# Gated delta rule in a decoder trunk: key and query norms as per-token factors, symmetric decayed products, and the next tile's front spread over the levels of this tile

## What is computed

```python
q = l2_norm(q) * (128 ** -0.5);  k = l2_norm(k)
g = cumsum(g) within the chunk                      # one decay per token and head
decay = exp(where(incl, g_i - g_j, -inf))
kb = k * beta
lower = where(strict, kb @ k.T * decay, 0)
rhs = concat([v * beta, kb * exp(g)])
u, w = triangular_solve(eye + lower, rhs)
attn = q @ k.T * decay
# over the chunks, S is the state (128 x 128 per head)
v_new = u - w @ S
o = (q * exp(g)) @ S + attn @ v_new
S = S * exp(g_last) + (k * exp(g_last - g)).T @ v_new
# then
o = rms_norm(o, onorm_w) * silu(z)
```

## Time and profile before

| | us |
|---|---|
| median of 3 runs (lowest, highest) | 2449.37 (2445.22, 2451.26) |
| the profiled execution's own time | 2451.56 |
| its span, first to last instruction | 2449.7 |
| PE busy | 2210.4 (90%) |
| DVE busy | 1598.6 (65%) |
| ACT busy | 1259.7 (51%) |
| POOL busy | 457.5 (19%) |
| mean granted TensorE clock, share of full speed | 0.949 |

### The profile page before, as it was taken

The page is one execution under the profiler, slowest core; times in us unless marked ns, Lnnn a source line. Parts: engine busy times, 40 slices in busy tenths (PEclk is TensorE's granted clock), DMA queues, the critical chain, the costliest instruction groups (busy, mean ns, idle before and its releaser), DMA issues. The chain is left out here.

```text
span 2449.7 us, 36342 instructions
## 1 busy us (share of the span) xinstructions
PE 2210.4 (90%) x10361; PEld 1679.8 (69%) x10361; DVE 1598.6 (65%) x2553; ACT 1259.7 (51%) x2072; POOL 457.5 (19%) x343
## 2 busy tenths in 40 slices
PE   7989688877999999999999399999999998999992
PEld 6867667776667776777777265567676776777771
DVE  3768754455578877788777321434777777888883
ACT  3332122122347777787776112322477776777871
POOL 0000322230013322232222000000132222322220
PEclk9999899998999999999999599699999999999996
DMA  5221000000469999999998502013699999999993
GB/s 190 87 86 39 18 1 1 1 1 19 173 225 376 373 360 348 359 376 367 361 357 289 172 26 69 1 39 132 230 366 340 365 351 342 372 364 372 372 348 94
DMA packets 177844, 536.68 MB, mean 219 GB/s; under 512 B 25856, under 2 KB 55520, under 8 KB 177632
## 3 DMA queue, kind: packets, MB, share of 16 engines
q1 hardware_dynamic: 147568, 457.50, 49.5%
q0 software_dynamic: 25248, 69.25, 11.3%
q10 hardware_dynamic: 4944, 8.84, 1.0%
HBM read 501.56 MB, written 54.07 MB: 227 GB/s over the span
## 5 line engine op out<-in xcount | busy, mean ns | idle before, releaser
L1322 DVE TENSOR_TENSOR gu_l<-ring,gu_h 128x1024 fp32r<-128x1024 f32 x512 | 611.3, 1221 | 99.5 <-ACT gu_h L1208 90.6
L1208 ACT CAST gu_h<-ring 128x1024 fp32r<-128x1024 f32 x512 | 523.3, 1058 | 91.7 <-DMA ring<-in_moe_w_up 74.3
L1140 PE MATMUL bank<-gu_h,xgT_l 128*128 128x512 f32 x1024 | 413.5, 404 | 0.0
L1142 PE MATMUL bank<-gu_h,xgT_h 128*128 128x512 f32 x1024 | 401.7, 392 | 0.0
L1141 PE MATMUL bank<-gu_l,xgT_h 128*128 128x512 f32 x1024 | 400.7, 391 | 0.0
L1450 POOL DMA_INDIRECT xg<-h_rows,list_idx x128 | 143.4, 1120 | 836.7 <-issue 318.2
L1179 PE MATMUL bank<-ring,hmT_f 128*128 128x512 f32 x544 | 279.3, 595 | 0.0
L1468 POOL DMA_INDIRECT moe_sum<-y,out_idx x128 | 216.1, 1688 | 220.2 <-issue 212.7
L1215 ACT CAST down_h<-ring 128x1024 fp32r<-128x1024 f32 x130 | 136.2, 1047 | 213.4 <-PE bank L1179 116.2
L1328 DVE TENSOR_TENSOR down_l<-ring,down_h 128x1024 fp32r<-128x1024 f32 x130 | 159.4, 1226 | 99.9 <-ACT down_h L1215 97.9
L1142 PEld LDWEIGHTS bank<-gu_h,xgT_h 128*128 128x128 f32 x1024 | 193.2, 189 | 42.6
(11 more groups left out here) (301 smaller groups left out, 3531.3 us busy)
## 6 DMA issues: line engine op xcount, KB each, us to landing
ring<-in_moe_w_gate SPq DMA_DIRECT2D x256, 512.0 KB
ring<-in_moe_w_up SPq DMA_DIRECT2D x256, 512.0 KB
ring<-in_moe_w_down SPq DMA_DIRECT2D x256, 512.0 KB
ring<-in_a_w_in SPq DMA_DIRECT2D x32, 512.0 KB
ring<-in_a_w_out SPq DMA_DIRECT2D x8, 512.0 KB
h_rows<-ring ACTq DMA_DIRECT2D x8, 512.0 KB, 2.7
moe_sum<-y ACTq DMA_DIRECT2D x8, 512.0 KB, 7.4
ring<-moe_sum SPq DMA_DIRECT2D x8, 512.0 KB, 5.5
```

Source lines behind the costliest of these rows:

```text
L1140: nc.tensor.matmul(out, lhsT=xl, rhs=wh, start=k == 0, stop=False)
L1142: last = nc.tensor.matmul(out, lhsT=xh, rhs=wh, start=False, stop=k == KD - 1)
L1208: nc.scalar.copy(gu_h[:, c, :, :], gate_up_cols(gate_slot, c * CH // 2, CH // 2)).then_inc(gu_hi.sem, 1)
L1322: nc.vector.tensor_tensor(gu_l[:, c, :, :], gate_up_cols(gate_slot, c * CH // 2, CH // 2), gu_h[:, c, :, :].bitcast(F32), ALU.subtract).th ...
```

## The change

The norms of q and k are no longer applied to q and k.

- The 16 `sum_squares` all add into one bank: a shifted row of one 1 as weights puts the sum of head c in row c. They are issued two after each of the first 8 z steps. One DVE copy, four PE transposes and a few operations on 128x32 or 128x64 elements give per token and head `k_gain` (beta over the sum), `k_norm` (root of the sum), `q_gain2` and `q_gain`. The 128x512 roots, reciprocals and scalings are gone.
- Decay is exp(-|g_i - g_j|), which is symmetric, so S = k k^T times decay serves as lower part and as its transpose, and the q by k product is made transposed at once (keys are the weights, key and query the 256 moving columns). The four transposes per group of L694 and L695 and the copies L759, L760 are gone. `k_gain` enters as a factor of rows (a matmul, `gain_rows`) and of columns, in `weighted`, and in the diagonal, in place of the identity (`diagonal`, on POOL). v is scaled by `k_norm`, the output by `q_gain` in `dve_gated`.
- X and Y of the next tile, and all that leads to them, are made during this tile: keys' transposes behind level 0, `gate_rows` behind level 1, `keys_queries` in two halves behind levels 2 and 3, `gain_rows` behind level 4, `first_X` and `first_Y` between the steps of the scan. Only tile 0 has a front of its own.
- Column sums of the decays are made once for all tiles (`cols`).
- In the scan, q by state stands ahead of the wait for v_new, four matmuls in a row, and attn by v_new follows as four in a row.
- POOL's order in a tile, two groups each, is now: `decay_queries`, mask 2, `scale_values`, mask 3, `upper_part` of the next tile, mask 4, `diagonal` of the next tile, then for each chunk c the decay of the state and mask c of the next tile. These are 22 operations a tile where there were 18.
- Semaphores that are no longer there for later blocks are shared with those of this one.

The diff, cut to its core (the removed PE, ACT, DVE and POOL programs of the block stand in the kernel above):

```diff
@@ gdn_projections, ScalarE
-                for c in range(2 * H + 1):
-                    if c < 2 * H:
-                        if c >= 2:
-                            act.wait_ge(side_ready.sem, side_ready.base + H + c - 1)
-                        nc.scalar.activation(squares[:, c % 2, :], qkT[:, c, :], ACT.Square).then_inc(squared.sem, 1)
-                    if c >= 1:
...
-                        nc.scalar.activation(norm[:, (c - 1) % 2, :], bank[6 + (c - 1) % 2][:, :], ACT.Sqrt, bias=eps_col[:, 0:1]).then_inc(norm_done.sem, 1)
+                for c in range(2 * H):
+                    if c >= 2:
+                        act.wait_ge(sums_ready.sem, sums_ready.base + c - 1)
+                    nc.scalar.activation(squares[:, c % 2, :], qkT[:, c, :], ACT.Square).then_inc(squared.sem, 1)
+                act.wait_ge(sums_copied.sem, sums_copied.base + 2)
+                nc.scalar.activation(k_norm[:, :, :], sum_cols[:, :, H:], ACT.Sqrt)
+                act.wait_ge(sums_copied.sem, sums_copied.base + 3)
+                nc.scalar.activation(q_gain[:, :, :], q_gain2[:, :, :], ACT.Sqrt, scale=float(P))
@@ gdn_projections, TensorE, behind each z step
-                    sum_squares(n)
+                    if n < H:
+                        if n == 0:
+                            pe.wait_ge(eps_set.sem, eps_set.base + 4)
+                        sum_squares(2 * n)
+                        sum_squares(2 * n + 1)
+                    elif n == H + 1:
+                        transpose_sums()
@@ gdn_projections, VectorE
-                for n in range(4 * TT + 1):
-                    if n < 4 * TT:
-                        copy_z(n)
-                    if n >= 1:
-                        normalise(n - 1)
+                for n in range(4 * TT):
+                    copy_z(n)
+                    if n == H:
+                        copy_sums()
+                    elif n == H + 2:
+                        norms()
@@ gdn_delta_rule, TensorE
+                def from_state(s, c):
...
+                    if c == 1:
+                        pe.wait_ge(vnew_done.sem, vnew_done.base + ev(s, 0) + 1)
+                    elif tt + 1 < TT:
+                        pe.wait_ge(w_scaled.sem, w_scaled.base + s + 3)
+                    for h in range(HG):
+                        last = nc.tensor.matmul(b[0][R, h * P:(h + 1) * P], lhsT=keg_wT[g][:, h, R], rhs=state[g][:, h, :], start=True, stop=True)
+                    last.then_inc(ws_ready.sem, 1)
...
+                    for h in range(HG):
+                        nc.tensor.matmul(b[3][R, h * P:(h + 1) * P], lhsT=qkT[:, HG * g + h, C], rhs=state[g][:, h, :], start=h == 0, stop=False)
+
+                def from_values(s, c):
...
+                    pe.wait_ge(vnew_done.sem, vnew_done.base + ev(s, c) + 1)
+                    for h in range(HG):
+                        nc.tensor.matmul(b[3][R, h * P:(h + 1) * P], lhsT=attnT[tt % 2][g][R, h, R], rhs=prod_vnew[g][R, h, :], start=False, stop=h == HG - 1)
+                    for h in range(HG):
+                        last = nc.tensor.matmul(b[1][:, h * P:(h + 1) * P], lhsT=k_dec[g][R, h, :], rhs=prod_vnew[g][R, h, :], start=True, stop=True)
+                    last.then_inc(scan_ready.sem, 1)
...
                 for tt in range(TT):
                     for level in range(LV):
+                        for s in both(tt):
+                            product(s, level)
+                        for s in both(tt):
+                            inverse(s, level)
+                        if level == 0:
+                            for s in both(tt):
+                                keys_T(s)
+                        elif tt + 1 < TT:
+                            for s in both(tt + 1):
+                                if level == 1:
+                                    gate_rows(s)
+                                elif level < 4:
+                                    keys_queries(s, level - 2)
+                                else:
+                                    gain_rows(s)
+                    for s in both(tt):
+                        values_keys(s)
+                    for c in range(2):
+                        for s in both(tt):
+                            from_state(s, c)
+                        for s in both(tt):
+                            from_values(s, c)
@@ gdn_delta_rule, ScalarE (decay(s) of the next tile follows the copies of level 2)
+                    nc.scalar.activation(eg_last[:, tt % 2, g, :, :], heads(b[0][:, :])[:, :, CHUNK - 1::CHUNK], ACT.Exp)
+                    nc.scalar.activation(eg_row[g][:, :, :], heads(b[0][:, :]), ACT.Exp)
+                    link(act, "act", nc.scalar.activation(sym[g], sym[g], ACT.Abs))
+                    nc.scalar.activation(sym[g], sym[g], ACT.Exp, scale=-1.0).then_inc(sym_done.sem, 1)
@@ gdn_delta_rule, VectorE
+                def decayed(s, half):
...
+                    v.wait_ge(kq_ready.sem, kq_ready.base + ev(s, half) + 1)
+                    v.wait_ge(sym_done.sem, sym_done.base + s + 1)
+                    both_of = kq_bank(s, half)[:, :].rearrange("p (h a q) -> p a h q", a=2, q=P)
+                    nc.vector.tensor_tensor(S[tt % 2][g][:, h, :], both_of[:, 1, :, :], sym[g][:, h, :], ALU.mult)
+                    v.wait_ge(upper_done.sem, upper_done.base + s + 1)
+                    nc.vector.tensor_tensor(attnT[tt % 2][g][:, h, :], both_of[:, 0, :, :], upper[g][:, h, :], ALU.mult).then_inc(kq_done.sem, 1)
+
+                def weighted(s):
...
+                    link(v, "dve", nc.vector.tensor_tensor(sym[g], heads(b_bank(s)[:, :]), S[tt % 2][g][:, :, :], ALU.mult))
+                    nc.vector.tensor_tensor(sym[g], sym[g], per_head(k_gain[:, tt, HG * g:HG * g + HG]), ALU.mult).then_inc(w_scaled.sem, 1)
+
+                def first_X(s):
...
+                    link(v, "dve", nc.vector.tensor_tensor(X[g][:, :, :], sym[g], planes(C_M0), ALU.mult))
+                    nc.vector.tensor_tensor(X[g][:, :, :], diag[g], X[g][:, :, :], ALU.subtract)
...
                     for c in range(2):
                         R = slice(c * CHUNK, (c + 1) * CHUNK)
+                        for s in both(tt):
+                            _, g, _, b = tile(s)
                             v.wait_ge(ws_ready.sem, ws_ready.base + ev(s, c) + 1)
+                            nc.vector.tensor_tensor(prod_vnew[g][R, :, :], v_tok[R, tt, HG * g:HG * g + HG, :], heads(b[0][R, :]), ALU.subtract).then_inc(vnew_done.sem, 1)
+                        if tt + 1 < TT:
+                            first_X(2 * tt + 2 + c)
+                        for s in both(tt):
+                            _, g, _, b = tile(s)
                             v.wait_ge(scan_ready.sem, scan_ready.base + ev(s, c) + 1)
                             v.wait_ge(state_decayed.sem, state_decayed.base + 2 + ev(s, c) + 1)
+                            nc.vector.tensor_tensor(state[g][:, :, :], sdec[g], heads(b[1][:, :]), ALU.add).then_inc(state_done.sem, 1)
+                        if tt + 1 < TT:
+                            first_Y(2 * tt + 2 + c)
@@ gdn_out, VectorE
-            nc.vector.tensor_scalar(o_rms[:, tt, :], o_rms[:, tt, :], 1.0 / P, EPS, ALU.mult, ALU.add).then_inc(rms_in.sem, 1)
+            nc.vector.tensor_tensor(o_rms[:, tt, :], o_rms[:, tt, :], q_gain2[:, tt, :], ALU.mult).then_inc(rms_in.sem, 1)
             v.wait_ge(rms_out.sem, rms_out.base + tt + 1)
             link(v, "dve", nc.vector.reciprocal(o_rms[:, tt, :], o_rms[:, tt, :]))
+            link(v, "dve", nc.vector.tensor_tensor(o_rms[:, tt, :], o_rms[:, tt, :], q_gain[:, tt, :], ALU.mult))
```

More of the change, by code:

```diff
@@ L661, in lev, with tile, both, kq_bank @@
             return 2 * per * tt + 2 * level + g
-        def banks(g):
-            return [bank[4 * g + i] for i in range(4)]
+        def tile(s):
+            tt, g = divmod(s, 2)
+            return tt, g, slice(tt * P, (tt + 1) * P), [bank[4 * g + i] for i in range(4)]
+        def both(tt):
+            return [2 * tt, 2 * tt + 1]
+        def kq_bank(s, half):
+            return tile(s)[3][1 + half if s < 2 else 0]
+        def b_bank(s):
+            return tile(s)[3][3 if s < 2 else 0]
+        def per_head(ap):
+            return ap.unsqueeze(2).to_broadcast([P, HG, P])
         with nc.Block(name="gdn_delta_rule") as block:
@@ new lines, in keys_queries @@
+                def keys_queries(s, half):
+                    tt, g, tok, b = tile(s)
+                    if tt > 0 and half == 0:
+                        pe.wait_ge(sym_done.sem, sym_done.base + s + 1)
+                    elif tt > 0:
+                        pe.wait_ge(kq_done.sem, kq_done.base + ev(s, 0) + 1)
+                    for j in range(2):
+                        h = HG * g + 2 * half + j
+                        last = nc.tensor.matmul(kq_bank(s, half)[:, 2 * j * P:2 * (j + 1) * P], lhsT=qkT[:, H + h, tok], rhs=qk_of[:, :, h, tok], start=True, stop=True)
+                    last.then_inc(kq_ready.sem, 1)
```

(34 more changed lines are left out.)

422 lines of the change are left out of this document (234 added, 188 removed).

## The result

| | us |
|---|---|
| changed kernel, median of 4 runs (lowest, highest) | 2375.38 (2371.89, 2375.94) |
| kernel before, median of 4 runs on the same chip | 2450.32 (2445.22, 2452.59) |
| ratio, 95% interval | 0.9694, 0.9676 to 0.9712 |
| the profiled execution's own time; its span | 2371.89; 2370.1 |

The change takes 74.9 us off. I had forecast 2386.0 (63.3 off) with a range of 2374 to 2408. Sign and range held, and what came is what I had called the rival of less contention and waiting, at 2376.

What follows compares the result with a forecast made beforehand. PE was taken as busy except in each tile's front, which DVE sets, so the front could be gained. Terms from projections to output stage summed to -63.3 us, against the median of 2449.37 giving 2386, range 2374 to 2408.

Steps and rivals of the forecast that it cites:

- less contention and waiting: Rival: POOL's gaps fall on first_X and first_Y, level 2 waits for nothing; 10 us less, 2376; chance 0.17.
- Projections: Norms and z steps: DVE loses its large norm operations, the block ends at 253.3 where it was 260.3; -7.0 us.
- Scan: Rows of four matmuls: a chunk takes 7.75 us where it was 10.3; last scan 16.4, -4.3 us for tile 3.
- Levels: Next tile's work between levels: +3.6 us each for tiles 1 and 2, +4.9 tile 0, -2.2 tile 3.
- Front of tile 0: Tile 0's open front, to the first inverse product: 27.3 us where it took 25.5; +1.8 us.
- Boundary: Scan start to next tile's first inverse product, three times: 20.9 us for 42.28; -21.4 each, -64.1 in all.
- The output stage: One more operation with its link, 0.2 us a tile, ahead of PE in two tiles: +0.4 us, between 0 and 0.9.
- PE's idle time: Sign to look for at the boundary: PE idle 2 to 4 us before the product of group 1, released by DVE's Y.
- The port on the critical chain: Rival: all SBUF operations of the boundary are blocked by POOL; 19 us, likely half: 2397; chance 0.15.
- The uncovered front: Rival: keys and queries wait in PE's strict order and levels stretch; +30 us, 2416; chance 0.10.
- PE's clock: Rival: the granted clock falls at the boundary and stays low, 32 us a tile; 2451 to 2514; chance 0.03.
- the second rival: The port on the critical chain: up to six more collisions of 1.06 us in three boundaries; 2397; chance 0.15.

Runs made afterwards that it cites:

- e2: Changed kernel with the next tile's front put back in series behind the scan on all engines, new formulas kept: 2433.39 us, ratio 0.9932 to the kernel before.
- e1: Changed kernel with q by state again behind the wait for v_new, alternating with attn by v_new: 2403.6 us, ratio 0.9817 to the kernel before.
- e4: Changed kernel, but in tile 0 POOL waits behind its first two masks for both `first_Y`: 2370.81 us, ratio 0.9696 to the kernel before.
- e7: Kernel of e4 with 14 POOL memsets of a scratch tile ahead of POOL's wait: 2369.19 us, ratio 0.9681 to the kernel before.
- e5: Changed kernel with POOL's `decay_queries` moved behind mask 2: 2379.24 us, ratio 0.9724 to the kernel before.
- e6: Changed kernel with four added POOL products on a scratch tile in the scan's second chunk: 2384.3 us, ratio 0.9727 to the kernel before.
- e11: Kernel of e8 with 9 filler matmuls (7 and 2) in place of 20: 2374.15 us, ratio 0.9674 to the kernel before.
- e8: Kernel of e4 with 20 unused filler matmuls on PE around tile 0's first products (16 and 4): 2378.2 us, ratio 0.9707 to the kernel before.

## Why the prediction was right, and where it was off

- **What bounds it.** The reading that the front is what can be gained, if PE has other work in it, held: e2 puts 54 of the 57 us it loses into the tile period.
- **Projections.** -6.99 for -7.0. The chain through PE, a last copy and the block's end was right.
- **Scan.** A chunk of 7.84 for 7.75, last scan 16.47 for 16.4. The cost of a change of shape was right (e1: 4.1 us of PE time for two chunks). That the same order covers DVE's `first_Y` ahead of v_new I had only as "v_new is ready behind the other group's products"; e1 gives it some 2.7 us a boundary, with the product's later release.
- **Levels.** 7.13 to 7.20 a level for 7.2. The step that failed is "In level 2 PE waits for ACT's two decays: +0.6": the second decay is done 1.7 us behind the first (295.15 and 296.88) where I had set 2.1, 6.05 us into the level for 6.9, and PE wants it at 6.3. With it go 0.6 of the 0.9 a tile by which tiles 1 and 2 came out shorter.
- **Front of tile 0.** The step that failed is the 27.3 us: 24.44. I had five of group 0's operations at 1.7; four are (1.63 to 1.75), `weighted` (L902) isn't. DVE's half products were also through at 9.0 us where I had 10.2. So group 0's product starts 17.2 us behind the start where I had Y ready at 20.0. Of group 1's operations two are lengthened (1.05 and 1.64). The mechanism was right, as e4 and e7 show; its count was too high, and some 1.2 of the 2.9 us come from the term ahead of it.
- **Boundary.** The step that failed is "Of six SBUF operations three or four pay 1.06, part of it hidden: first_Y at 20.0, inverse at 20.9". Collisions do occur (1.42, 1.55, 1.64), but all of them ahead of the last state, under PE's matmuls, and the inverse comes at 18.94, 0.2 behind the 18.7 that I had worked out for a POOL that is away. Up to the end of the delta rule the ledger has -74.6 and my terms -63.7: of these 10.9 us the boundaries are 5.9, the front of tile 0 2.8 and the levels 2.2. The output stage goes the other way by some 0.7. My argument for 20.9, that DVE and POOL took turns wherever both had work, didn't ask when POOL would have work: its mask of level 2 stands behind a PE product. e5 shows how near the other outcome is: one swap in POOL's order brings the collision onto `first_Y`.
- **PE's idle time** before the product of group 1 was to be 2 to 4 us and is 0.70, for the same reason.
- **The rivals.** Less contention and waiting is what happened (2376 forecast by it, 2375.38 measured). I had given it a chance of 0.17. That it fits to under 1 us is luck in part: the runs spread over 4 us, and its 10 us were set as 6.6, 1.8 and 2 where the stages show 5.9, 2.2 and 2.8. The port on the critical chain didn't happen, but e6 makes it happen with more POOL work. The uncovered front didn't: no wait inside a level of tiles 0 to 2. PE's clock stayed at 1.00 in every boundary of the changed kernel, and e6 shows that the concern was real: with a wait of 2.38 us in place of 0.70 it fell at two of three boundaries, and behind the last it was back at 1.00 over 452 to 458: a short fall, not the lasting one that would have made the kernel slower than before.
- **Slips in the working.** The 2397 of the second rival doesn't follow from half of 19 us, which gives some 2395.5. (1.16 - 0.28) us belongs to seven records, not eight; the 0.111 us that I took is what the runs show all the same (eight records in 0.88 us).
- **The whole.** The stages that the change touches give 73.9 up to the first mixture, which is 1 less than the medians' 74.9.

## What to carry to other kernels

When the front of the next step can be cut into pieces that fit behind the levels of this one, most of its length is gained, as long as no piece is late: of e2's 25.3 us in series the spreading saved some 18 a tile. The rest comes back as 3.3 us of products at the boundary and as longer levels. The pieces may even be dearer in series than those they replace (25.3 us for 21.6 here). To price two engines that take turns on SBUF, don't multiply collisions by their cost: find, for each, what releases the other engine at that moment, and whether PE has work left. An order of PE that puts what is ready ahead of what waits for DVE pays twice, in the waits as well as in the shapes.

## What the runs showed that I had not expected

- A POOL that is busy for 8.09 us with memsets leaves DVE's operations with two SBUF inputs at 0.69; masks and products make them 1.63 to 1.75.
- Taking a collision away in one place made the boundary longer (e5: 19.8 us for 18.94), since the work behind it moved up onto the chain.
- A longer wait of PE at a boundary (2.38 us) costs more than itself where the granted clock then falls: at the last boundary the product of group 1 took 2.08 us for 1.16, and from its start to level 1 it was 8.19 us for 5.45 (e6).
- The clock in tile 0's front could be held at 1.00 by 9 matmuls whose results aren't used, and level 1 then began 2.35 us earlier (e11); with 20 of them it began 4.8 us later (e8).
